# Rotary partner rows: eight TensorE products per layer replaced by copies between SBUF rows

## The chip, the cores and the metric

One core of a Trainium2 chip runs the whole program as one launch. The metric is the device time of that launch in microseconds. The kernel before was run three times; the median is 3442.33 us. One further execution was taken with the profiler, and its rows are the ones read here.

## What is computed

The reference is a stack of transformer layers over 512 tokens of width 1024, in f32: two layers of one block (their mixers are the kernel's `even` and `odd` phases, each between two feed-forward phases) and two layers of a second block. The change is in the token mixer of the second block, the kernel's `mix2` phase, which runs twice. Cut to what matters:

```
def apply_axial_rope(x, cos, sin):          # d = 64 (grouped heads) or 32 (latent heads)
    d = x.shape[-1]; h = d // 2; q = h // 2
    xr, xc = x[..., :h], x[..., h:]
    rot = lambda z: concatenate([-z[..., q:], z[..., :q]], axis=-1)
    x_rot = concatenate([rot(xr), rot(xc)], axis=-1)
    return x * cos + x_rot * sin

def token_mixer(u, ...):
    qa, ka, va, cq, ckv, kr, gl = split(u @ w_in)
    qa = apply_axial_rope(rmsnorm(qa, q_norm_g), cos_a, sin_a)      # 8 heads of 64
    ka = apply_axial_rope(rmsnorm(ka, k_norm_g), cos_a, sin_a)      # 2 heads of 64
    ya = blocked_attention(qa, ka, va)
    q_nope, q_rope = split(rmsnorm(cq, q_a_norm_g) @ w_q_up)        # 8 heads of 64 + 32
    k_nope, vb     = split(rmsnorm(ckv, kv_a_norm_g) @ w_kv_up)
    yb = blocked_attention([q_nope, rope(q_rope)], [k_nope, rope(kr)], vb)
    return merge of (ya, yb) with sigmoid gates, times w_o
```

The rotary step needs, for every row of a query or key, its partner row: 16 rows away for a head of 64, 8 rows away for a head of 32, with a sign.

## The kernel before

Activations lie with features on the 128 SBUF rows (partitions) and the 512 tokens along the free dimension, so one head pair is a tile of 128 x 512. Every f32 weight product is three TensorE passes: the weight block is split by ScalarE into a rounded high part (`round_to`, L381) and by GpSimd into the rest (`rest_block`, L408); SyncE loads the blocks (`load`, L360) through a ring of six slots. A load waits until TensorE is done with the block six places earlier, and `round_ahead` lets ScalarE round five blocks ahead of the item in hand, so at each item ScalarE waits for a load that starts when the block of the item before is done.

The front part of `mix2` follows a list written by hand, `ORDER2` (its rows stand below with the code), which all engines walk in the same order:

- `cq`, `kv`, `qk`, `kr`, `va`: projections of the input, one weight block each (three passes over eight row blocks on TensorE at L419 to L421). VectorE copies each result out of PSUM with the norm's factor (`b_qk` at L2503, `b_kr` at L2508, `b_vt` at L2510).
- `sum`: sums of squares for the norms, small matmuls at L2255 and L2258, from squares that ScalarE makes (L2417). After the third and the last `sum` ScalarE takes a square root (L2396) and VectorE a reciprocal (L2488).
- `spread`: the inverse norms of the latents and of the grouped keys spread over rows; VectorE applies them.
- `rot` 0 to 3 (grouped queries), `rot` 4 (grouped keys), `rotkr` (shared rotary key), `rotup` 0 and 1 (rotary part of the latent queries): the rotary step. TensorE multiplies the tile by a 128 x 128 matrix of signs (L2299: `b_rot` for the queries, which holds the norm's gain as well, or a part of `b_tab`) into one of five PSUM banks; VectorE multiplies that by the sine table into `work` (L2541), multiplies the tile by the cosine table in place (L2544 or L2547) and adds (L2548). That is eight rotary steps in a layer, sixteen in the program.
- `upr`, `upn`, `kn`: the latent queries and keys from their ranks (L2310 to L2312, L2321 to L2323), copied out by VectorE (L2555, L2561). `turn` transposes the grouped values.

PSUM is used in turn: a product that goes to tile n waits until VectorE has copied out tile n - 5 (`acc_free`). At the end TensorE waits for the copy of the last `kn` tile and for all eight rotary steps, and starts the attention (L1255), whose first operands ScalarE rounds (L2387) and VectorE splits (L2565). ScalarE issues no DMA in this phase; in the whole program it issues four, at the start.

Of the kernel before, what the change touches and what calls it, by code (L numbers as in the profile page):

```python
# [22 lines left out]
P = 128  # L23
S = 512
# [150 lines left out]
def build(nc, t, stop=99):  # L175
    with ExitStack() as ctx:
# [65 lines left out]
        mid2 = [("b_qk", [P, RAWS, S], F32), ("b_va", [P, S], F32), ("b_rot", [P, P], F32), ("gap2", [P, 2 * S - P], F32)]  # L242
        b_tab, b_small, c_hi, c_lo, b_qk, b_va, b_rot, _, b_qn, b_qr, b_kn, b_kr, b_vb = over(
# [48 lines left out]
        side_done, raw_copied, rotated = sem("side_done"), sem("raw_copied"), sem("rotated")  # L292
        tables_loaded, odd_loaded = sem("tables_loaded"), sem("odd_loaded")
# [1839 lines left out]
        COS_A, SIN_A, COS_B, SIN_B, ROT_A, ROT_B = 0, S, 2 * S, 3 * S, 4 * S, 4 * S + P  # L2133
# [12 lines left out]
        ROTS2 = [item for item in ORDER2 if item[0] in ("rot", "rotkr", "rotup")]  # L2146
        SIDES2 = 3 + 1
# [40 lines left out]
        def mix2_sp(sp, c, i):  # L2188

            def tables():  # L2190
                sp.wait_ge(blocks_done, block_done(c.blocks - 1))
                sp.dma_start(b_tab[:], t["tab_b"]).then_inc(tables_loaded, 16)
# [12 lines left out]
        def mix2_end(c):  # L2205
            c.blocks += len(mix2_blocks())
            c.tiles += len(TILES2)
            c.add("side", SIDES2 + len(ROTS2))
# [30 lines left out]
        def mix2_pe(pe, c, e):  # L2239
# [23 lines left out]
            for kind, i in ORDER2:  # L2263
# [206 lines left out]
        def mix2_dve(dve, ch, c):  # L2470
# [5 lines left out]
            for kind, i in ORDER2:  # L2476
# [8 lines left out]
                if kind == "sum":  # L2485
# [3 lines left out]
                    if i == GQ + 3:  # L2489
                        dve.wait_ge(rstd2_ready, c.at("rstd2") + 2)  # L2490
                        ch.link(dve.tensor_scalar(stat[:, 1, 8:40], stat[:, 0, 0:32], -HD ** -0.5, None, ALU.mult))
                        ch.link(dve.tensor_scalar(stat[:, 0, 0:32], stat[:, 0, 0:32], HD ** -0.5, None, ALU.mult))
                if kind in STEPS2:
# [6 lines left out]
                if (kind, i) == ("qk", 4):  # L2500
                    ch.link(dve.tensor_scalar(b_rot[:], b_tab[:, ROT_A:ROT_A + P], b_small[:, 0:1], None, ALU.mult))
# [33 lines left out]
                elif kind in ("rot", "rotkr", "rotup"):  # L2535
                    side, rots = side + 1, rots + 1
                    dst, _ = rotated_tile(kind, i)
                    cos, sin = (COS_A, SIN_A) if kind == "rot" else (COS_B, SIN_B)
                    dve.wait_ge(side_done, side)
                    dve.wait_ge(rotated, rots - 1)  # L2540
                    dve.tensor_tensor(work[:, 0, :], src[:], b_tab[:, sin:sin + S], ALU.mult).then_inc(acc_drained, 1)  # L2541
                    if kind == "rot" and i < 4:
                        dve.wait_ge(x_squared, c.at("sq") + NORMS2.index(("qk", i)) + 1)
                        ch.link(dve.scalar_tensor_tensor(out=dst, in0=dst, scalar=b_small[:, 0:1],  # L2544
                                                         in1=b_tab[:, COS_A:COS_A + S], op0=ALU.mult, op1=ALU.mult))
                    else:
                        ch.link(dve.tensor_tensor(dst, dst, b_tab[:, cos:cos + S], ALU.mult))  # L2547
                    dve.tensor_tensor(dst, dst, work[:, 0, :], ALU.add).then_inc(rotated, 1)  # L2548
# [287 lines left out]

def rotation(n, width, first=0):
# [5 lines left out]
    return r  # L2843


def second_table():
# [8 lines left out]
    a, b = np.tile(angles(HD), (2, 1)), angles(32)  # L2855
    b = np.tile(b, (4, 1))
    return np.concatenate([np.cos(a), np.sin(a), np.cos(b), np.sin(b), rotation(P, 32), rotation(P, 16)], 1).astype(f)


def lay_out(a):  # L2860
# [50 lines left out]
    a_cols = np.concatenate([np.arange(HD) + HD * head for j in range(4) for head in (j, j + 4)])  # L2911
    ins, ups, kvs, gates, outs, smalls, fup, fdown = ([] for _ in range(8))
    for i in range(2):
        w = a["w_in_2"][i]
        kr = np.tile(w[:, 1408:1440], (1, 4))
        ins.append(tiles_of(np.concatenate([w[:, 768:1408], w[:, 512:640], w[:, a_cols], kr, w[:, 640:768]], 1)))
        up = a["w_q_up_2"][i].reshape(QR * P, 8, QK)
        nope, rope = np.split(tiles_of(np.concatenate([up[:, :, :HD].reshape(QR * P, -1), up[:, :, HD:].reshape(QR * P, -1)], 1)), [4])
# [8 lines left out]
        smalls.append(np.concatenate([np.tile(a["q_norm_g_2"][i], 2)[:, None], np.tile(a["k_norm_g_2"][i], 2)[:, None],  # L2927
                                      columns(a["q_a_norm_g_2"][i]), columns(a["kv_a_norm_g_2"][i]),
                                      np.zeros((P, 1), np.float32), columns(a["b_gate_2"][i])], 1))
# [20 lines left out]
```

## Time and profile before

| | |
|---|---|
| median of three runs | 3442.33 us (3440.7 to 3442.33) |
| the profiled execution, whole | 3441.55 us |
| its span, first to last instruction | 3439.7 us |
| TensorE busy | 3400.9 us, 99% of the span |
| VectorE, GpSimd, ScalarE busy | 2087.8 us, 1989.7 us, 1530.3 us |
| granted TensorE clock, mean | 0.998 |

The front parts of `mix2` that the change touches lie at about 2000 to 2074 us and 2729 to 2805 us from the span's start. The program waits for TensorE nearly everywhere, so an instruction taken off TensorE counts fully unless TensorE then waits for something else. Matmuls overlap at their ends, so what one costs is read from the distance of starts. In the profile each f32 rotary matmul appears as two (x2).

### The profile page before, as it was taken

The numbers are of one execution on the slowest core, as the hardware profiler recorded it, in microseconds if no ns is written. First come the engines' busy times: TensorE is split into PE (matmuls) and PEld (weight loads), VectorE is DVE, ScalarE is ACT, GpSimd is POOL, SyncE is SP. The second block draws the span as 40 slices with busy tenths as digits, with TensorE's granted clock in tenths as the row PEclk, the third lists the DMA queues.
The fourth block names the chain that finished last, engine by engine and source line by source line (L and its number), as shares of the span: only waits on it lengthen the run. The fifth ranks groups of instructions, "written<-read, shape, count | busy, mean of one in ns | idle before, by whom it ended". The sixth has DMA issues, their size and how long they took to land. (4 is left out here: it accounts for less than half of the span.)

```text
span 3439.7 us, 46281 instructions
## 1 busy us (share of the span) xinstructions
PE 3400.9 (99%) x17572; PEld 2761.2 (80%) x17572; DVE 2087.8 (61%) x2990; ACT 1530.3 (44%) x2388; POOL 1989.7 (58%) x2338
## 2 busy tenths in 40 slices
PE   9999999999999999999999999999999999999999
PEld 8888868888888888748888887788788876888887
DVE  5556666655764468766645667326767575238667
ACT  4334454333533355675333537434444555335444
POOL 6555645555655658745665557554655665546564
PEclk9999999999999999999999999999999999999999
DMA  4223203233222322202332220123222210232321
GB/s 173 89 77 117 85 20 118 79 110 111 86 98 91 130 70 93 71 1 83 123 111 103 83 76 26 56 92 123 98 98 92 86 59 8 93 105 92 114 107 62
DMA packets 87726, 301.56 MB, mean 88 GB/s; under 512 B 9936, under 2 KB 14544, under 8 KB 87120
## 3 DMA queue, kind: packets, MB, share of 16 engines
q1 hardware_dynamic: 85392, 296.50, 24.4%
q8 instruction: 140, 2.29, 0.3%
q10 hardware_dynamic: 2112, 2.10, 0.2%
q14 instruction: 82, 0.67, 0.1%
HBM read 296.46 MB, written 2.10 MB: 87 GB/s over the span
## 5 line engine op out<-in xcount | busy, mean ns | idle before, releaser
L408 POOL TENSOR_TENSOR w_lo<-w_raw,w_hi 128x256 fp32r<-128x256 f32 x1754 | 1364.6, 812 | 1091.5 <-ACT w_hi L381 841.9
L419 PE MATMUL bank<-xh,w_hi 128*128 128x512 f32 x2544 | 997.8, 392 | 3.9 <-issue 1.5
L421 PE MATMUL bank<-xh,w_lo 128*128 128x512 f32 x2544 | 989.2, 389 | 0.0
L420 PE MATMUL bank<-xl,w_hi 128*128 128x512 f32 x2544 | 989.2, 389 | 0.0
L381 ACT ACTIVATE w_hi<-w_raw 128x1024 fp32r<-128x1024 f32 (+2 forms) x485 | 498.5, 1039 | 671.3 <-DMA w_raw<-in_ffn_up 269.3
L419 PEld LDWEIGHTS bank<-xh,w_hi 128*128 128x128 f32 x2544 | 478.1, 188 | 106.5 <-issue 4.6
L420 PEld LDWEIGHTS bank<-xl,w_hi 128*128 128x128 f32 x2544 | 478.2, 188 | 99.7 <-issue 2.4
L421 PEld LDWEIGHTS bank<-xh,w_lo 128*128 128x128 f32 x2544 | 478.0, 188 | 99.5
L408 POOL TENSOR_TENSOR extra_lo<-extra_raw,w_hi 128x256 fp32r<-128x256 f32 x264 | 229.8, 905 | 126.1 <-ACT w_hi L381 113.1
L1099 DVE TENSOR_TENSOR y_tok<-y_tok,bank 128x512 f32<-128x512 f32 x232 | 157.4, 685 | 223.1 <-PE bank L978 223.1
L1133 DVE TENSOR_TENSOR work<-bank,sqsum 128x512 f32<-128x512 f32 x88 | 60.7, 690 | 267.7 <-PE bank L421 267.7
L1025 ACT ACTIVATE ph<-work 128x1024 fp32r<-128x1024 f32 x76 | 80.7, 1062 | 299.1 <-DVE work L1113 299.1
L1379 POOL TENSOR_TENSOR work<-work,red 128x1024 f32<-128x1024 f32 (+2 forms) x88 | 151.3, 1721 | 88.5 <-DVE red L1325 88.5
L976 PE MATMUL bank<-w_hi,ph 128*128 128x512 f32 x512 | 200.0, 391 | 1.5 <-DVE work L1140 1.5
L978 PE MATMUL bank<-w_hi,pl 128*128 128x512 f32 x512 | 199.3, 389 | 0.0
L408 POOL TENSOR_TENSOR extra_lo<-extra_raw,x_hi 128x256 fp32r<-128x256 f32 x120 | 130.8, 1125 | 47.8 <-ACT x_hi L381 47.8
L381 ACT ACTIVATE w_hi<-extra_raw 128x1024 fp32r<-128x1024 f32 (+1 forms) x98 | 95.1, 1000 | 110.9 <-PE bank L978 107.4
L976 PE MATMUL bank<-w_hi,sh 128*128 128x512 f32 x360 | 140.5, 390 | 2.0 <-DVE sl L1121 1.2
L978 PE MATMUL bank<-w_hi,sl 128*128 128x512 f32 x360 | 140.1, 389 | 0.0
L1309 DVE TENSOR_REDUCE red<-scores 128x2 f32<-128x1024 f32 (+2 forms) x88 | 97.9, 1112 | 60.4 <-PE scores L1277 40.7
L642 PE MATMUL bank<-xh,w_hi 128*128 128x256 f32 x480 | 126.9, 293 | 2.4 <-ACT xh L602 2.4
L643 PE MATMUL bank<-xh,w_lo 128*128 128x256 f32 x480 | 123.3, 286 | 0.0
(454 smaller groups left out, 6154.2 us busy)
## 6 DMA issues: line engine op xcount, KB each, us to landing
w_raw<-in_ffn_up SPq DMA_DIRECT2D x176, 512.0 KB, 3.5
w_raw<-in_b_ffn_up SPq DMA_DIRECT2D x64, 512.0 KB, 3.5
extra_raw<-in_ffn_down SPq DMA_DIRECT2D x52, 512.0 KB, 4.5
w_raw<-in_b_gates SPq DMA_DIRECT2D x48, 512.0 KB, 3.4
extra_raw<-in_b_ffn_down SPq DMA_DIRECT2D x40, 512.0 KB, 4.5
w_raw<-in_od_in SPq DMA_DIRECT2D x33, 512.0 KB, 3.5
w_raw<-in_b_in SPq DMA_DIRECT2D x24, 512.0 KB, 3.6
w_raw<-in_ffn_down SPq DMA_DIRECT2D x20, 512.0 KB, 3.4
```

The lines of the kernel that those rows point to most:

```text
L381: act.activation(hi_of(g, whole(g)), src, ACT.Copy).then_inc(w_rounded, 1)
L408: ins = pool.tensor_tensor(lo_of(g, part), raw_of(g, part), hi_of(g, part).bitcast(F32), ALU.subtract)
L419: pe.matmul(out, wh, hi, start=first, stop=False)
L420: pe.matmul(out, wh, lo, start=False, stop=False)
L421: return pe.matmul(out, wl, hi, start=False, stop=last)
L642: pe.matmul(out, hi_of(B + j, cols), xh[:, k, half(h)], start=k == 0, stop=False)
L643: pe.matmul(out, lo_of(B + j, cols), xh[:, k, half(h)], start=False, stop=False)
L976: pe.matmul(out[:], hi, hi_of(block, cols), start=opens, stop=False, skip_group_check=True)
L978: mm = pe.matmul(out[:], lo, hi_of(block, cols), start=False, stop=ends, skip_group_check=True)
L1099: ins = dve.tensor_tensor(to, to, src, ALU.add)
L1309: ch.link(dve.reduce_max(r[:, 0:2], scores[g % 2][:, :, 0:u["keys"]], mybir.AxisListType.X))
L1379: pool.tensor_tensor(p, p, red[:, g % 4, 8:10].unsqueeze(2).broadcast_to([P, 2, u["keys"]]), ALU.mult)\
```

## The change

The eight rotary products of a layer leave TensorE. In their place ScalarE issues DMAs that copy each group of rows of the tile to the partner's rows of a new buffer `b_partner`, two tiles of 128 x 512 used in turn, and VectorE multiplies this by a sine table that now holds the sign. On the host the columns of the query and key weights (with their gains and tables) are put in another order, so that partners are 32 rows apart in a head of 64 and 16 in a head of 32: a `rot` tile takes four copies of 32 rows (64 KB each), the three others eight copies of 16 rows (32 KB each), 44 in a layer. Two semaphores, one for each buffer, count the landings. `MOVE_AT` names the item at which ScalarE issues each move; before a move it waits for the tile to be copied out and, from the third move on, for the rotary step two before. VectorE's three instructions of a step, and their place in `ORDER2`, stay; the first reads SBUF instead of PSUM. The product that made `b_rot` goes, and the table load loses the two sign matrices. ScalarE's rounding of the first grouped operands moves from the item `rotup` 0 to the item `upn` 1, behind the last move. The rotary tiles no longer take a turn in the five PSUM banks.

```
-        mid2 = [("b_qk", [P, RAWS, S], F32), ("b_va", [P, S], F32), ("b_rot", [P, P], F32), ("gap2", [P, 2 * S - P], F32)]
+        mid2 = [("b_qk", [P, RAWS, S], F32), ("b_va", [P, S], F32), ("b_partner", [P, 2, S], F32)]
...
-        STEPS2 = ("sum", "add")
+        STEPS2 = ("sum", "add", "rot", "rotkr", "rotup")
...
+        MOVE_AT = {("rot", 0): ("qk", 1), ("rot", 1): ("qk", 2), ("rot", 4): ("qk", 3), ("rot", 2): ("kr", 0), ("rotkr", 0): ("va", 0),
+                   ("rot", 3): ("va", 0), ("rotup", 0): ("upr", 1), ("rotup", 1): ("upn", 0)}
...
-                elif kind in ("rot", "rotkr", "rotup"):
-                    src, made = rotated_tile(kind, i)
-                    turn = b_rot[:] if kind == "rot" and i < 4 else b_tab[:, ROT_A:ROT_A + P] if kind == "rot" else \
-                        b_tab[:, ROT_B:ROT_B + P]
-                    pe.wait_ge(acc_drained, acc_free(tile))
-                    pe.wait_ge(acc_drained, drained(c.tiles + TILES2.index(made)))
-                    pe.wait_ge(tables_loaded, 48 + 32 * (c.at("tables") + 1))
-                    pe.matmul(out, turn, src, start=True, stop=True).then_inc(side_done, 1)
...
+            def move(r):
+                src, made = rotated_tile(*ROTS2[r])
+                wide = HD // 2 if ROTS2[r][0] == "rot" else 16
+                act.wait_ge(acc_drained, drained(T + TILES2.index(made)))
+                if r >= 2:
+                    act.wait_ge(rotated, c.at("rotated") + r - 1)
+                for to in range(0, P, wide):
+                    at = to + wide if to // wide % 2 == 0 else to - wide
+                    act.dma_start(b_partner[to:to + wide, r % 2, :], src[at:at + wide, :]).then_inc(partner_moved[r % 2], 16)
...
-                if (kind, i) == ("rotup", 0):
+                if (kind, i) == ("upn", 1):
                     act.wait_ge(rotated, c.at("rotated") + ROTS2.index(("rot", 3)) + 1)
                     round_grouped(act, 4)
                     round_grouped(act, 0)
...
                     round_ahead(act, g + (1 if g < c.blocks + OPEN else 0))
                     g += 1
+                for r, item in enumerate(ROTS2):
+                    if MOVE_AT[item] == (kind, i):
+                        move(r)
...
+                if kind in ("rot", "rotkr", "rotup"):
+                    r = ROTS2.index((kind, i))
+                    dst, _ = rotated_tile(kind, i)
+                    cos, sin = (COS_A, SIN_A) if kind == "rot" else (COS_B, SIN_B)
+                    dve.wait_ge(partner_moved[r % 2], moves(L, r))
+                    dve.wait_ge(rotated, rots)
...
+                        ch.link(dve.tensor_tensor(work[:, 0, :], b_partner[:, r % 2, :], b_tab[:, sin:sin + S], ALU.mult))
+                        ch.link(dve.tensor_tensor(dst, dst, b_tab[:, cos:cos + S], ALU.mult))
+                    dve.tensor_tensor(dst, dst, work[:, 0, :], ALU.add).then_inc(rotated, 1)
```

The order of instructions shows it at two places. The first is TensorE at the end of the fourth query projection of the first `mix2`, before:

```order
L420 MATMUL bank<-xl,w_hi 128x512
L421 MATMUL bank<-xh,w_lo 128x512
L2299 MATMUL bank<-b_qk,b_tab 128x512
L2258 MATMUL bank<-meancol,work 128x2 x4
L419 MATMUL bank<-xh,w_hi 128x512
```

and in the changed kernel (its lines are numbered a little higher):

```order
L421 MATMUL bank<-xl,w_hi 128x512
L422 MATMUL bank<-xh,w_lo 128x512
L2266 MATMUL bank<-meancol,work 128x2 x4
L420 MATMUL bank<-xh,w_hi 128x512
L421 MATMUL bank<-xl,w_hi 128x512
```

The rotary product of the grouped keys is gone, and the sums of squares follow the projection directly. The second place is ScalarE from the square of the last query tile to the rounding of the grouped operands, before (L381 rounds a weight block, L2396 is the square root of the last sums):

```order
L2417 ACTIVATE work<-b_qk 128x512
L381 ACTIVATE w_hi<-w_raw 128x1024 x2
L2396 ACTIVATE stat<-bank 128x32
L381 ACTIVATE w_hi<-w_raw 128x1024 x2
L2387 ACTIVATE hi_a<-b_qk 128x512 x2
```

and in the changed kernel:

```order
L2430 ACTIVATE work<-b_qk 128x512
L382 ACTIVATE w_hi<-w_raw 128x1024
L2402 DMA b_partner<-b_qk 32x512 x4
L382 ACTIVATE w_hi<-w_raw 128x1024
L2402 DMA b_partner<-b_kr 16x512 x8
L2402 DMA b_partner<-b_qk 32x512 x4
L2406 ACTIVATE stat<-bank 128x32
L382 ACTIVATE w_hi<-w_raw 128x1024
L2402 DMA b_partner<-b_qr 16x512 x8
L382 ACTIVATE w_hi<-w_raw 128x1024
L2402 DMA b_partner<-b_qr 16x512 x8
L2387 ACTIVATE hi_a<-b_qk 128x512 x2
```

Thirty-two DMA issues now stand between ScalarE's own instructions here, twelve of them directly ahead of the square root.

## Rows read from the trace of the kernel before

**Rows 1.** The page's busy times, all engines, whole span.

```profile
PE 3400.9 (99%) x17572; PEld 2761.2 (80%) x17572; DVE 2087.8 (61%) x2990; ACT 1530.3 (44%) x2388; POOL 1989.7 (58%) x2338
```

**Rows 2.** TensorE's waits, first `mix2` front and the attention's start.

```profile
PE scores L1255 <- DVE b_kn L2561: 0.8, 1, 0.8
PE bank L2258 <- ACT work L2417: 0.8, 1, 0.8
```

**Rows 3.** Timeline, TensorE, first layer: start us, us, engine, line, operation [idle <-releaser].

```profile
2035.93 1.02 PE L2299 MATMUL bank<-b_qk,b_tab 128*128 128x512 f32 x2
2036.79 0.95 PE L2258 MATMUL bank<-meancol,work 128*128 128x2 f32 x8
...
2062.65 1.02 PE L2299 MATMUL bank<-b_qr,b_tab 128*128 128x512 f32 x2
...
2063.74 0.40 PE L2311 MATMUL bank<-c_lo,w_hi 128*128 128x512 f32 x1
2063.97 0.40 PE L2312 MATMUL bank<-c_hi,w_lo 128*128 128x512 f32 x1
...
2072.84 0.39 PE L2323 MATMUL bank<-c_hi,w_lo 128*128 128x512 f32 x1
2074.02 0.50 PE L1255 MATMUL scores<-hi_a 64*128 64x512 f32 x2 [0.78 <-DVE b_kn L2561]
```

**Rows 4.** Timeline, VectorE, first layer, the last rotary step to the attention.

```profile
2063.87 0.68 DVE L2541 TENSOR_TENSOR work<-bank,b_tab 128x512 f32<-128x512 f32 x1
2064.47 0.72 DVE L2547 TENSOR_TENSOR b_qr<-b_qr,b_tab 128x512 f32<-128x512 f32 x1
2065.22 1.12 DVE L2548 TENSOR_TENSOR b_qr<-b_qr,work 128x512 f32<-128x512 f32 x1
2066.26 0.68 DVE L2555 COPY b_qn<-bank 128x512 f32<-128x512 f32 x1
...
2073.27 0.69 DVE L2561 COPY b_kn<-bank 128x512 f32<-128x512 f32 x1 [0.65 <-PE bank L2323]
```

**Rows 5.** Timeline, ScalarE, first layer.

```profile
2021.23 0.63 ACT L2417 ACTIVATE work<-b_qk 128x512 f32<-128x512 f32 x1 [4.79 <-DVE b_qk L2503]
...
2046.83 1.06 ACT L381 ACTIVATE w_hi<-w_raw 128x1024 fp32r<-128x1024 f32 x1 [6.23 <-DMA w_raw<-in_b_kv]
2051.38 0.20 ACT L2396 ACTIVATE stat<-bank 128x32 f32<-128x32 f32 x1 [3.49 <-PE bank L2258]
2054.57 1.06 ACT L381 ACTIVATE w_hi<-w_raw 128x1024 fp32r<-128x1024 f32 x1 [2.99 <-DMA w_raw<-in_b_gates]
2060.92 1.06 ACT L381 ACTIVATE w_hi<-w_raw 128x1024 fp32r<-128x1024 f32 x1 [5.29 <-DMA w_raw<-in_b_gates]
```

**Rows 6.** Timeline, DMA issues of ScalarE's queue.

```profile
0.71 2.57 ACTq L2742 DMA_DIRECT2D x<-in_x  x4
```

**Rows 7.** Timeline, DMA issues of SyncE's queue, two stretches.

```profile
2043.35 0.33 SPq L360 DMA_DIRECT2D w_raw<-in_b_kv  x1
...
2359.55 1.87 SPq L360 DMA_DIRECT2D extra_raw<-in_b_ffn_down  x4
```

**Rows 8.** DMA issues by line: count, KB each, median us from issue to landing.

```profile
w_raw<-in_b_kv SPq DMA_DIRECT2D x4, 512.0 KB, 3.5
out_x<-x SPq DMA_DIRECT2D x16, 128.0 KB, 1.8
w_raw<-in_ffn_down SPq DMA_DIRECT2D x4, 256.0 KB, 2.5
b_small<-in_b_small SPq DMA_DIRECT2D x2, 12.0 KB, 6.8
```

**Rows 9.** Stretches (us; busy by engine; last three: granted clock, DMA share, GB/s).

```profile
2013.00:2076.00 63.00, 61.44 (x297) 47.97 (x297) 39.80 (x58) 20.18 (x29) 30.59 (x39) 1.00 0.23 77
2742.00:2806.00 64.00, 62.44 (x295) 48.75 (x294) 39.31 (x59) 19.91 (x28) 29.86 (x38) 0.97 0.22 73
...
2744.00:2748.00 4.00, 4.00 (x12) 3.08 (x12) 0.25 (x1) 1.12 (x3) 4.00 (x7) 0.57 0.00 0
```

More of the change, by code:

```diff
@@ L241, in build @@
         head2 = [("c_hi", [P, QR + KR, S], F32R), ("c_lo", [P, QR + KR, S], F32R)]
-        mid2 = [("b_qk", [P, RAWS, S], F32), ("b_va", [P, S], F32), ("b_rot", [P, P], F32), ("gap2", [P, 2 * S - P], F32)]
-        b_tab, b_small, c_hi, c_lo, b_qk, b_va, b_rot, _, b_qn, b_qr, b_kn, b_kr, b_vb = over(
+        mid2 = [("b_qk", [P, RAWS, S], F32), ("b_va", [P, S], F32), ("b_partner", [P, 2, S], F32)]
+        b_tab, b_small, c_hi, c_lo, b_qk, b_va, b_partner, b_qn, b_qr, b_kn, b_kr, b_vb = over(
             "hh", *tab2, *head2, *mid2, ("b_qn", [P, 4, S], F32), ("b_qr", [P, 2, S], F32), ("b_kn", [P, 4, S], F32),
@@ L292, in build @@
         side_done, raw_copied, rotated = sem("side_done"), sem("raw_copied"), sem("rotated")
+        partner_moved = [sem(f"partner_moved{i}") for i in range(2)]
         tables_loaded, odd_loaded = sem("tables_loaded"), sem("odd_loaded")
@@ L2146, in build, with moves, pieces @@
         ROTS2 = [item for item in ORDER2 if item[0] in ("rot", "rotkr", "rotup")]
+        MOVE_AT = {("rot", 0): ("qk", 1), ("rot", 1): ("qk", 2), ("rot", 4): ("qk", 3), ("rot", 2): ("kr", 0), ("rotkr", 0): ("va", 0),
+                   ("rot", 3): ("va", 0), ("rotup", 0): ("upr", 1), ("rotup", 1): ("upn", 0)}
+        def moves(layer, r):
+            def pieces(item):
+                return 4 if item[0] == "rot" else 8
+            return 16 * (layer * sum(map(pieces, ROTS2[r % 2::2])) + sum(map(pieces, ROTS2[r % 2:r + 1:2])))
         SIDES2 = 3 + 1
@@ L2207, in mix2_end @@
             c.tiles += len(TILES2)
-            c.add("side", SIDES2 + len(ROTS2))
+            c.add("side", SIDES2)
             c.add("rotated", len(ROTS2))
@@ L2492, in mix2_dve @@
                         ch.link(dve.tensor_scalar(stat[:, 0, 0:32], stat[:, 0, 0:32], HD ** -0.5, None, ALU.mult))
+                if kind in ("rot", "rotkr", "rotup"):
[4 more added lines that the diff above has]
+                    dve.wait_ge(rotated, rots)
+                    rots += 1
+                    if kind == "rot" and i < 4:
+                        ch.link(dve.scalar_tensor_tensor(out=work[:, 0, :], in0=b_partner[:, r % 2, :], scalar=b_small[:, 7:8],
+                                                         in1=b_tab[:, SIN_A:SIN_A + S], op0=ALU.mult, op1=ALU.mult))
+                        dve.wait_ge(x_squared, c.at("sq") + NORMS2.index(("qk", i)) + 1)
+                        ch.link(dve.scalar_tensor_tensor(out=dst, in0=dst, scalar=b_small[:, 0:1],
+                                                         in1=b_tab[:, COS_A:COS_A + S], op0=ALU.mult, op1=ALU.mult))
+                    else:
+                        ch.link(dve.tensor_tensor(work[:, 0, :], b_partner[:, r % 2, :], b_tab[:, sin:sin + S], ALU.mult))
+                        ch.link(dve.tensor_tensor(dst, dst, b_tab[:, cos:cos + S], ALU.mult))
+                    dve.tensor_tensor(dst, dst, work[:, 0, :], ALU.add).then_inc(rotated, 1)
                 if kind in STEPS2:
@@ L2534, in mix2_dve @@
                     dve.wait_ge(xl_ready, xn + j + 1)
[L2535 to L2548, printed above, removed]
                 elif kind in ("upr", "upn"):
@@ L2834, in even_table, with turn_sign @@
     return np.concatenate([np.cos(ang), np.sin(ang), mask, pool, rotation(P, HD)], 1).astype(f)
+def turn_sign(width):
+    return np.where(np.arange(P) % width < width // 2, -1, 1)[:, None]
 def rotation(n, width, first=0):
@@ L2843, in rotation, with turned_order @@
     return r
+def turned_order(dim):
+    return np.arange(dim).reshape(2, 2, dim // 4).transpose(1, 0, 2).reshape(-1)
 def second_table():
@@ L2854, in angles @@
         return np.concatenate([r, r, c, c], 1).T.astype(f)
-    a, b = np.tile(angles(HD), (2, 1)), angles(32)
+    a, b = np.tile(angles(HD)[turned_order(HD)], (2, 1)), angles(32)[turned_order(32)]
     b = np.tile(b, (4, 1))
-    return np.concatenate([np.cos(a), np.sin(a), np.cos(b), np.sin(b), rotation(P, 32), rotation(P, 16)], 1).astype(f)
+    return np.concatenate([np.cos(a), turn_sign(HD) * np.sin(a), np.cos(b), turn_sign(32) * np.sin(b)], 1).astype(f)
 def lay_out(a):
@@ L2911, in lay_out @@
     a_cols = np.concatenate([np.arange(HD) + HD * head for j in range(4) for head in (j, j + 4)])
+    order_a, order_b = turned_order(HD), turned_order(32)
+    q_cols = np.concatenate([order_a + HD * head for j in range(4) for head in (j, j + 4)])
+    k_cols = np.concatenate([512 + order_a + HD * head for head in range(2)])
     ins, ups, kvs, gates, outs, smalls, fup, fdown = ([] for _ in range(8))
@@ L2914, in lay_out @@
         w = a["w_in_2"][i]
-        kr = np.tile(w[:, 1408:1440], (1, 4))
-        ins.append(tiles_of(np.concatenate([w[:, 768:1408], w[:, 512:640], w[:, a_cols], kr, w[:, 640:768]], 1)))
+        kr = np.tile(w[:, 1408 + order_b], (1, 4))
+        ins.append(tiles_of(np.concatenate([w[:, 768:1408], w[:, k_cols], w[:, q_cols], kr, w[:, 640:768]], 1)))
         up = a["w_q_up_2"][i].reshape(QR * P, 8, QK)
-        nope, rope = np.split(tiles_of(np.concatenate([up[:, :, :HD].reshape(QR * P, -1), up[:, :, HD:].reshape(QR * P, -1)], 1)), [4])
+        nope, rope = np.split(tiles_of(np.concatenate([up[:, :, :HD].reshape(QR * P, -1), up[:, :, HD + order_b].reshape(QR * P, -1)], 1)), [4])
         ups.append(np.concatenate([rope, nope]).transpose(1, 0, 2).reshape(P, -1))
@@ L2926, in lay_out @@
         outs.append(tiles_of(a["w_o_2"][i]))
-        smalls.append(np.concatenate([np.tile(a["q_norm_g_2"][i], 2)[:, None], np.tile(a["k_norm_g_2"][i], 2)[:, None],
+        q_gain, k_gain = a["q_norm_g_2"][i][order_a], a["k_norm_g_2"][i][order_a]
+        smalls.append(np.concatenate([np.tile(q_gain, 2)[:, None], np.tile(k_gain, 2)[:, None],
                                       columns(a["q_a_norm_g_2"][i]), columns(a["kv_a_norm_g_2"][i]),
-                                      np.zeros((P, 1), np.float32), columns(a["b_gate_2"][i])], 1))
+                                      np.tile(np.roll(q_gain, HD // 2), 2)[:, None], columns(a["b_gate_2"][i])], 1))
         fup.append(tiles_of(a["w_ffn_up_2"][i]))
```

6 lines of the change are left out of this document (2 added, 4 removed).

## The prediction

> **What bounds the kernel now.** I read the page's busy times first: TensorE is busy 99% of the span, the others 44 to 61% [rows 1]. So the kernel is TensorE's list of instructions, and what leaves it is a gain as long as TensorE finds no new wait. The waits come next: in the front of the first `mix2` TensorE waits twice, 0.8 us each, once for a square and once, ahead of the attention, for VectorE's copy of the last latent keys [rows 2]; the second layer has the same two. VectorE and ScalarE follow so closely that the front is near a second bound, and that is what the timelines are read for. The last matmul of the front and the first of the attention show the 0.78 us of waiting [rows 3]. VectorE's last rotary step ends at 2066.3, its last copy starts at 2073.27 as soon as its product is there, and ScalarE idles for 3 to 6 us between its weight roundings, most of it for loads [rows 4, 5].
>
> **What leaves TensorE.** One rotary product takes 2036.79 - 2035.93 = 0.86 us between starts; where a projection follows, the second matmul behind it stands 1.09 us later, and less one step of 0.23 that is 0.86 again [rows 3]. Read so, the eight of a layer cost 0.86 to 0.95, 7.15 us in all, and the sixteen 14.3 us. If nothing else changed the front would end 7.15 us earlier in each layer. The product that made `b_rot` (once a layer) stands ahead of several us of idle VectorE time and counts as nothing; if that time were gone it would cost what a short VectorE instruction costs. The shorter table load counts as nothing too: it is issued before the mixer's projections.
>
> **What ScalarE gets.** In a layer five moves of four DMAs and three of eight. No row shows an issue of 16 or 32 rows of SBUF, so the price is bounded by the nearest ones. SyncE's single issue takes 0.33 us and four in a row take 1.87, 0.47 each [rows 7]; ScalarE's own four, of larger pieces at the start, take 2.57, 0.64 each [rows 6]. I take 0.37 for the first and 0.44 for each further one: nearest to SyncE's four in a row, a little less because a piece has a quarter or an eighth of the rows, if rows matter. That is 1.7 us for four, 3.45 for eight. Ends for the range: 0.33 and 0.64. For the landing I take 1.8 us from the start of the last issue, the row of 128 KB [rows 8]; sizes of 256 and 512 KB take 2.5 and 3.5, so little is left to gain with size. Below, a landing of 1.0 would give 0.8 us more a layer; above stands the 6.8 us of a 12 KB load that was queued behind a large one.
>
> Here the Trainium skill speaks otherwise: "DMA: Bandwidth & Descriptors", under "Issuing engines are not separate DMA queues", says that the sequencer's time to start a DMA is usually small relative to the DMA itself. By that rule the sum would be the whole 14.3 us. The rows speak against it for pieces as small as these: four issues together take as long as one landing [rows 6 to 8].
>
> **The path.** I followed the engines' lists in order with these durations (without the change this reproduces the first layer's front within 0.3 us). VectorE's own three instructions per step stay, 2.5 us with their gaps [rows 4]; the first now reads SBUF only, and I give it 0.1 us more.
>
> The moves of `rot` 0 and 1 are hidden: ScalarE idles 4.79 us ahead of a square there [rows 5]; without it the square, and the sums behind it, would come 1.7 us later. Those of `rot` 4 and 2 land about 0.9 us after VectorE is ready, which VectorE's idle time ahead of the next two projections takes up.
>
> From `va` on it binds. TensorE is now 3.6 us early. ScalarE rounds the block whose load starts at the end of `kr`: before at 2046.83 [rows 5], now at about 2044.1, done at 2045.1. Then come twelve issues, 5.15 us, and the square root behind them runs at 2050.3 instead of 2051.38, though its sums are ready at 2047.6: 2.5 of the 3.6 us are lost. Behind it VectorE waits, since the reciprocal stands ahead of its `rotkr` step, that ahead of the copy of `upr` 0, and this is what ScalarE's next move waits for. The copy is done at 2054.1; eight issues to 2057.6, landed at 2058.9, half a us after VectorE needs them; `rotup` 0 done at 2061.5. ScalarE rounds a block (1.06) and issues the last eight from 2058.6 to 2062.0, landed at 2063.4; VectorE has waited 1.3 us, and ends the last step at 2065.9, hardly earlier than the 2066.3 of before. What is gained comes behind it: eight instructions of about 0.62 us that were spread over TensorE's `kn` products, up to 2073.27 [rows 4], now follow each other, and end at 2070.9. TensorE meanwhile stands twice, 2.2 us ahead of its last `kn` tile (the copy of five tiles before is late) and 3.0 us behind it. The attention begins at about 2071.2 instead of 2074.02 [rows 3]: 2.8 us gained per layer of the 7.15.
>
> **The clock.** In the second layer TensorE's granted clock was 0.57 in one stretch of 4 us, 1.2 instead of 2.4 GHz for most of it, and not in the first, where the whole front shows 1.00 [rows 9]. Ahead of that fall stood small matmuls and the 0.8 us wait. It cost 0.43 of 4 us, 1.7 us. The 2.2 and 3.0 us waits with one short product between them leave TensorE idle for longer, so I count a fall at the attention's start in each layer: 3.4 us. Bounds: none (0), or these and no second-layer fall (-1.7 more gained).
>
> **The sum**, against the profiled execution's own time, which is 0.78 us under the median: 3441.55 - 2 x 2.8 + 2 x 1.7 = 3439.3 us. The attention and all behind it are the same list of instructions; the turn of the five banks shifts, but no wait on a bank shows there.
>
> **Rivals.** All are measured against the median; about 0.2%, 6.9 us, is what a measurement of this kernel can tell from no change.
>
> *The issues cost next to nothing*, and ScalarE's moves vanish between its roundings. Then VectorE is never late and TensorE gains all: 3441.55 - 14.3 = 3427.3 us. For it: ScalarE's idle time and the small pieces. Against it: the four issues in a row of either queue [rows 6, 7]. Chance 0.15. The rule of the Trainium skill quoted above would have it so.
>
> *Slower: ScalarE's issues cost what its own row says*, 0.64 each. Place: the twelve issues ahead of the square root (7.7 us) and the two eights (5.1 us each) behind it, one chain through VectorE. The same walk gives 2.85 us lost per layer, with the two falls of the clock 3441.55 + 5.7 + 3.4 = 3450.7 us. It decides from about 0.49 us per issue, where gain and clock cancel. For it: it is this engine's only row [rows 6]. Against it: those were 512 KB pieces, issued while SyncE issued six. Chance 0.14.
>
> *The landings are late*, because the copies share the 16 engines with weight loads of 3.5 us [rows 8]. At 4 us a layer loses 0.3: 3445.6 us with the falls; at 5.2 it loses 3.6: 3452.2 us. For it: a weight load is under way in about half the front. Against it: the copies have ScalarE's own queue, and each is small. Chance 0.18.
>
> **How the numbers follow.** The forecast, chance 0.53, covers issues of 0.37 to 0.48 us, 4.4 to 1.9 us per layer, with none to two falls: 3432.7 to 3441.2 us. Faster by over 0.2% (below 3435.4) are the first rival and a fifth of the forecast: 0.26. Slower by over 0.2% (above 3449.2) are most of the second and about 0.07 of the third: 0.20. The rest, 0.54, is within. The range, 3429 to 3451, leaves out the first rival's end and the worst landings: issues of 0.33 (5.8 per layer) without a fall give 3430.0, the slow rival 3450.7.
>
> **What would show it.** Right: rows of four and eight issues on ScalarE's queue of 1.5 to 1.9 and 3.2 to 3.8 us; the second square root about 1 us earlier while its sums stand ready; VectorE waiting for DMA ahead of its last two steps; TensorE waiting some 2 and 3 us at the last `kn` tile and the attention; a granted clock well under 1 there. Wrong: no new wait on TensorE (first rival), issues of 0.6 us, or landings of 4 us and more.

## The result, and the profile after

The changed kernel takes 3449.44 us (median of 16 runs, 3447.66 to 3452.38) against 3442.19 us (16 runs, 3440.13 to 3444.07) for the kernel before in the same comparison: ratio 1.0021, 95% interval 1.0014 to 1.0029. It is slower by 7.25 us, a little more than the 0.2% that the prediction named as measurable, and not 3 us faster. The profiled execution took 3447.66 us with a span of 3445.9 us.

The page's busy times after, to be held against [rows 1]:

```profile
PE 3390.6 (98%) x17540; PEld 2755.2 (80%) x17540; DVE 2090.1 (61%) x2988; ACT 1530.0 (44%) x2388; POOL 2000.2 (58%) x2338
```

TensorE works 10.3 us less than before and the span is 6.2 us longer, so some 16 us of new waiting replaced the products. TensorE's waits in the first `mix2` front of the changed kernel (us in total, times, longest) show where:

```profile
PE bank L2321 <- DVE b_qn L2569: 4.7, 2, 2.7
PE scores L1256 <- DVE b_kn L2575: 2.7, 1, 2.7
PE bank L2310 <- DVE b_qr L2569: 2.6, 2, 1.6
PE bank L2266 <- ACT work L2430: 0.8, 1, 0.8
```

Before there were two waits of 0.8 us [rows 2]. Now there are 10.0 us ahead of VectorE's copies, more than the 7.15 us of products that went. VectorE is late because ScalarE is. ScalarE's timeline in the changed kernel, from the item `va` on:

```profile
2043.96 4.99 ACTq L2402 DMA_DIRECT2D b_partner<-b_kr  x8
2049.05 3.44 ACTq L2402 DMA_DIRECT2D b_partner<-b_qk  x4
2052.53 0.20 ACT L2406 ACTIVATE stat<-bank 128x32 f32<-128x32 f32 x1 [7.85 <-issue]
...
2057.18 5.00 ACTq L2402 DMA_DIRECT2D b_partner<-b_qr  x8
2062.22 1.06 ACT L382 ACTIVATE w_hi<-w_raw 128x1024 fp32r<-128x1024 f32 x1 [8.55 <-DVE b_qn L2569]
2062.30 5.00 ACTq L2402 DMA_DIRECT2D b_partner<-b_qr  x8
```

Eight issues take 5.0 us. The square root (L2406) waits for nothing but the issues ahead of it: TensorE's last sums of squares began at 2045.84 and took 0.95 us, the root ran at 2052.53. VectorE's timeline in the same stretch shows what follows from it:

```profile
2052.76 0.35 DVE L2501 RECIPROCAL stat<-stat 128x32 f32<-128x32 f32 x1 [5.70 <-ACT stat L2406]
...
2063.60 1.05 DVE L2520 TENSOR_TENSOR work<-b_partner,b_tab 128x512 f32<-128x512 f32 x1 [1.91 <-DMA b_partner<-b_qr]
...
2068.71 0.69 DVE L2520 TENSOR_TENSOR work<-b_partner,b_tab 128x512 f32<-128x512 f32 x1 [1.19 <-DMA b_partner<-b_qr]
2069.43 0.69 DVE L2521 TENSOR_TENSOR b_qr<-b_qr,b_tab 128x512 f32<-128x512 f32 x1
2070.16 1.10 DVE L2522 TENSOR_TENSOR b_qr<-b_qr,work 128x512 f32<-128x512 f32 x1
2071.18 1.27 DVE L2569 COPY b_qn<-bank 128x512 f32<-128x512 f32 x2
...
2074.91 1.28 DVE L2575 COPY b_kn<-bank 128x512 f32<-128x512 f32 x2
```

It stands 5.70 us for the reciprocal and 1.91 and 1.19 us for the landings of the last two moves. The last rotary step ends at 2071.3 (2066.3 before, [rows 4]), the last copy at 2076.2. TensorE's timeline:

```profile
2067.58 0.50 PE L2321 MATMUL bank<-c_hi,w_hi 128*128 128x512 f32 x1 [1.97 <-DVE b_qn L2569]
2071.92 0.49 PE L2321 MATMUL bank<-c_hi,w_hi 128*128 128x512 f32 x1 [2.68 <-DVE b_qn L2569]
2076.24 0.49 PE L1256 MATMUL scores<-hi_a 64*128 64x512 f32 x2 [2.67 <-DVE b_kn L2575]
```

The span can be cut where TensorE starts the third sum of squares (`sum` GK, the last point that the moves cannot reach) and where it starts the attention, in each layer:

| stretch, us | before | after | difference |
|---|---|---|---|
| start to sums, layer 1 | 2013.82 | 2012.63 | -1.2 |
| front, sums to attention, layer 1 | 60.20 | 63.61 | +3.4 |
| attention to sums, layer 2 | 668.84 | 671.93 | +3.1 |
| front, layer 2 | 61.79 | 64.26 | +2.5 |
| attention of layer 2 to the end | 635.05 | 633.47 | -1.6 |

The two fronts lose 5.9 us together. Of the 3.1 us between them 1.6 are a clock fall right behind the attention's start: from 2078.5 to 2081.1 TensorE's starts stand 0.43 us apart instead of 0.23 (the stretches from 2076 to 2084 below), and the second scores follow the first after 6.09 us instead of 4.53. Another 1.5 us are an idle gap of TensorE with no releaser, which is not the change's: each of the eleven profiles has it once, behind one of the two attentions. In the changed kernel it stands behind the first, in the kernel before behind the second, where it makes the -1.6 of the last row:

```profile
2192.84 0.47 PE L420 MATMUL bank<-xh,w_hi 128*128 128x512 f32 x1 [1.47 <-issue]
```

```profile
2919.86 0.47 PE L419 MATMUL bank<-xh,w_hi 128*128 128x512 f32 x1 [1.47 <-issue]
```

The -1.2 of the first row lies ahead of the moves, and nothing here explains it.

### The profile page after: what moved, and what is told of

It reads as the page before. It is cut to its first block, busy times and chain, and to the rows that moved or that the text cites. A ratio compares the mean times of both kernels' runs of the same rounds, so it can differ in the third digit from the quotient of the medians.

```text
span 3445.9 us, 46307 instructions
## 1 busy us (share of the span) xinstructions
PE 3390.6 (98%) x17540; PEld 2755.2 (80%) x17540; DVE 2090.1 (61%) x2988; ACT 1530.0 (44%) x2388; POOL 2000.2 (58%) x2338
## 4 chain that ended last, share of the span: by engine, by line
PE 48%; DVE 5%; POOL 2%; ACTq 1%; issue 1%; ACT 1%; DMA 0%; DVEq 0%; POOLq 0%
PE bank L420 9%; PE bank L422 9%; PE bank L421 9%; PE bank L977 3%; PE bank L979 3%; PE bank L978 3%; PE bank L1294 2%; PE bank L1271 2%; PE scores L1256 2%; POOL extra_lo L409 2%; ACTq L2402 1%; PE bank L2366 1%; PE bank L2367 1%; PE bank L2368 1%; PE bank L1747 1%
```

## The experiments

The theory: ScalarE's price of an issue, about 0.61 us, 44 times a layer, made the loss. Rival 1: the way out of VectorE's tile through a DMA and back costs what it costs, however many pieces and whoever issues. Rival 2: only the falls of the clock in TensorE's new waits count. The kernel before ran beside each; every ratio is to it.

| kernel | median us (range, runs) | before | ratio, 95% interval |
|---|---|---|---|
| e1 two issues a move | 3431.47 (3428.13 to 3437.62, 7) | 3441.83 | 0.9973, 0.9962 to 0.9983 |
| e2 issued by SyncE | 3442.87 (3440.1 to 3447.26, 11) | 3441.83 | 1.0005, 0.9996 to 1.0015 |
| e3 64 issues a layer | 3460.99 (3459.09 to 3463.32, 5) | 3441.83 | 1.0057, 1.0044 to 1.007 |
| e4 `rot` alone | 3432.17 (3431.36 to 3433.11, 7) | 3441.83 | 0.9972, 0.9961 to 0.9983 |
| e5 `rot` 3 behind the root | 3446.82 (3445.03 to 3449.92, 11) | 3442.16 | 1.0014, 1.0006 to 1.0023 |
| e6 waits filled | 3447.51 (3444.51 to 3448.74, 11) | 3442.16 | 1.0014, 1.0006 to 1.0023 |
| e7 e1 + `kn` copies by ScalarE | 3431.42 (3430.3 to 3432.92, 5) | 3442.16 | 0.9968, 0.9955 to 0.998 |
| e8 `rotkr`, `rotup` alone | 3452.42 (3451.1 to 3455.34, 7) | 3442.16 | 1.0029, 1.0018 to 1.004 |
| e9 e1 + `upn` copies by ScalarE | 3427.93 (3425.43 to 3428.18, 5) | 3441.3 | 0.9961, 0.9948 to 0.9975 |

**e1, the same bytes in 16 issues a layer instead of 44.**

```
-    return np.arange(dim).reshape(2, 2, dim // 4).transpose(1, 0, 2).reshape(-1)
+    return np.arange(dim).reshape(2, 2, dim // 4).transpose(0, 2, 1).reshape(-1)
...
-                for to in range(0, P, wide):
-                    at = to + wide if to // wide % 2 == 0 else to - wide
-                    act.dma_start(b_partner[to:to + wide, r % 2, :], src[at:at + wide, :]).then_inc(partner_moved[r % 2], 16)
+                for s in range(2):
+                    act.dma_start(b_partner[s:P:2, r % 2, :], src[1 - s:P:2, :]).then_inc(partner_moved[r % 2], 16)
```

> The order of the columns is changed once more, so that a row's partner is the next row (the sine table's signs and the gains follow). A move is then two DMAs by ScalarE, 64 rows each at a step of two rows, instead of four or eight: 16 issues in a layer instead of 44, with the same bytes, the same issuing engine and the same places. Theory (ScalarE's issue price, 0.61 us each, is what turned the gain into a loss): ScalarE is rid of 28 x 0.61 = 17 us per layer, VectorE is no longer late, and nearly all of the 14.3 us of rotary products comes out: 3428 us, up to 3431.5 if TensorE's clock still falls. Rival 1 (the way out and back counts, VectorE to DMA to VectorE, 2.1 us however many pieces): as the change, 3447 to 3450. Rival 2 (only the clock falls count): not below 3442 as long as TensorE waits at the start of the attention.

Measured 3431.47 us, at the theory's upper figure, and 3428.13 in the profiled execution. Rival 1 falls: the moves still go out through a DMA and back. ScalarE's timeline of e1 at the place of the twelve issues:

```profile
2043.16 1.12 ACTq L2400 DMA_DIRECT2D b_partner<-b_kr  x2
2044.55 1.12 ACTq L2400 DMA_DIRECT2D b_partner<-b_qk  x2
2046.73 0.20 ACT L2404 ACTIVATE stat<-bank 128x32 f32<-128x32 f32 x1 [2.56 <-PE bank L2266]
```

The root now waits for TensorE's sums and not for issues, and comes 5.8 us earlier. Of TensorE's waits in the front two are left, 0.8 and 1.7 us. Rival 2's "not below 3442" falls too. The spread of 9.5 us goes with the mean granted clock of the runs, 0.999 in the fastest and 0.996 in the slowest; where the falls lay, the one profile, taken in the fastest run, cannot show.

**e2, the 44 pieces issued by SyncE.** The move's body stands in SyncE's list, each behind a weight load:

```
+            behind = {0: [0], 1: [1], 2: [2], 3: [3], 4: [4, 5], 5: [6], 6: [7]}
...
+                load(sp, g + j, src)
+                for r in behind.get(j, []):
+                    move(r)
```

> The same 44 pieces in a layer, issued by SyncE: each move directly behind the weight load that SyncE issues at about that time; it waits there for the same two semaphores. ScalarE has no moves. Theory: SyncE issues these pieces in 0.33 to 0.47 us each, so with landings of 2.1 us the front gains 2.0 us per layer, 3442.2 - 4.0 + 3.4 (clock) = 3441.6 us; with landings of 4 us, if a piece waits behind the 512 KB load ahead of it in the same queue, 0.7 us lost per layer, 3447. In both cases the second square root comes as soon as its sums are ready. Rival 1 (the way out and back): 3447 to 3450, with the square root early and VectorE just as late. If the price belongs to the piece (SBUF to SBUF, 16 or 32 rows) and not to the engine, SyncE's rows show 0.61 too and the time is as the change, 3449.

The expectation was wrong on the price and the time lay at its smaller figure. SyncE's timeline of e2:

```profile
2043.46 4.93 SPq L2213 DMA_DIRECT2D b_partner<-b_kr  x8
2048.49 2.43 SPq L2213 DMA_DIRECT2D b_partner<-b_qk  x4
2050.97 1.59 SPq L361 DMA_DIRECT2D w_raw<-in_b_gates  x1
2054.19 4.93 SPq L2213 DMA_DIRECT2D b_partner<-b_qr  x8
2059.17 0.58 SPq L361 DMA_DIRECT2D w_raw<-in_b_gates  x1
```

Eight issues cost SyncE 4.93 us, hardly less than ScalarE's 5.0; even a weight load right behind them costs 0.58, once 1.59, instead of the 0.33 of [rows 7]. So the price is not ScalarE's own. The expectation's last case had this price, but a time as the change's with it, and the time did not follow. What the issuer decides is who stands behind the issues. Here ScalarE's root was punctual (2048.93, released by TensorE's sums), and VectorE waited 2.42 and 2.87 us for the landings of the two `rotup` moves; the kernel gains 6.6 us on the change and ends level with the kernel before. In exchange the weight loads stand behind the moves: ScalarE's rounding waits up to 6.5 us for one, without holding TensorE up.

**e3, 20 more issues a layer.**

```
-                for to in range(0, P, wide):
+                for to in range(0, P, 16):
...
-                    act.dma_start(b_partner[to:to + wide, r % 2, :], src[at:at + wide, :]).then_inc(partner_moved[r % 2], 16)
+                    act.dma_start(b_partner[to:to + 16, r % 2, :], src[at:at + 16, :]).then_inc(partner_moved[r % 2], 16)
```

> The five rot moves of a layer in eight pieces of 16 rows instead of four of 32: 20 more issues per layer by ScalarE, the same bytes, places and waits otherwise. Theory: 20 x 0.61 = 12.2 us more on ScalarE per layer, of which some 8 us reach the path (the walk through the lists): 3449.4 + 16 = 3465 us. Rival 1: a move comes back as before, 3448 to 3452. Rival 2: as the change, since TensorE's number of waits is the same, 3449 to 3452.

Measured 3460.99 us, 11.6 us above the change for 40 more issues; both rivals said none. The size, 16 us expected, was too large. In the profiled executions the spans are 13.3 us apart; the fronts, 68.28 and 69.27 us, are 4.7 and 5.0 above the change's, where the theory had some 8 each. (The second difference is 6.6 without a clock fall of 1.6 us at the third sum of squares, which the change has in that layer and e3 has not; see e6.) The rows of the pieces (count, ns as min, median and max), first of the change and then of e3, say that halving a piece does not cheapen it:

```profile
L2402 ACTq DMA_DIRECT2D b_partner<-b_qk x40: 514/612/1576, 2014.2 to 2787.8; - x40
```

```profile
L2402 ACTq DMA_DIRECT2D b_partner<-b_qk x80: 514/611/1301, 2015.5 to 2798.6; - x80
```

and in e1, with 64 rows in a piece, it is not dearer:

```profile
L2400 ACTq DMA_DIRECT2D b_partner<-b_qk x20: 472/559/932, 2014.2 to 2769.6; - x20
```

**e4 and e8, one half of the change each.** In e4 the five `rot` steps are moved and the rest are products again; in e8 it is the other way round. The core of e4, and of e8:

```
-        STEPS2 = ("sum", "add", "rot", "rotkr", "rotup")
+        STEPS2 = ("sum", "add", "rot")
+        MOVED2 = [item for item in ROTS2 if item[0] == "rot"]
```

```
-        STEPS2 = ("sum", "add", "rot", "rotkr", "rotup")
+        STEPS2 = ("sum", "add", "rotkr", "rotup")
+        MOVED2 = [item for item in ROTS2 if item[0] != "rot"]
```

> Only the five rot steps of a layer (grouped queries and keys) are moved, four issues each by ScalarE as in the change; rotkr and the two rotup steps are TensorE products again, with the column order of before for the latent heads. Theory: the 20 issues lie beside ScalarE's idle time and none stands ahead of the last two steps, so the five products come out, 4.5 us per layer: 3442.2 - 9.0 = 3433.2 us. Rival 1 (way out and back): rot 2 and rot 3 are still late by a landing each; VectorE makes up for that, 3433 to 3436. Rival 2 (clock): the waits at the attention's start are short as in the kernel before, so no fall there: 3433. If the first five moves already cost what they save, 3442.

> The converse of moving the five rot steps alone: these are TensorE products again (with the column order of before for the heads of 64), and rotkr and the two rotup steps are moved, eight issues each by ScalarE, 24 in a layer. Theory: eight issues stand ahead of the second square root, and rotup's two eights each on the path between a copy and VectorE's step; by the walk 3.1 us lost per layer although three products are gone: 3442.2 + 6.2 = 3448.4, up to 3452 with clock falls at the attention's start. Rival 1 (the way out and back): 3442 to 3446. If the five rot moves carried the loss: 3437, the three products saved.

Measured 3432.17 us for e4 (expected 3433.2) and 3452.42 us for e8 (expected 3448.4, up to 3452 with clock falls). The 20 issues for `rot` are covered by ScalarE's idle time; the 24 of the other three steps are not, and cost more than the whole change. TensorE's waits in the first front of e4 are those of before:

```profile
PE scores L1256 <- DVE b_kn L2588: 0.8, 1, 0.8
PE bank L2265 <- ACT work L2435: 0.8, 1, 0.8
```

VectorE's timeline of e8 shows it late at each of the three moves, and not mainly for the root:

```profile
2052.66 0.35 DVE L2507 RECIPROCAL stat<-stat 128x32 f32<-128x32 f32 x1 [0.80 <-ACT stat L2412]
2055.87 0.69 DVE L2518 TENSOR_TENSOR work<-b_partner,b_tab 128x512 f32<-128x512 f32 x1 [2.42 <-DMA b_partner<-b_kr]
2066.68 1.10 DVE L2518 TENSOR_TENSOR work<-b_partner,b_tab 128x512 f32<-128x512 f32 x1 [3.31 <-DMA b_partner<-b_qr]
2071.55 0.69 DVE L2518 TENSOR_TENSOR work<-b_partner,b_tab 128x512 f32<-128x512 f32 x1 [0.90 <-DMA b_partner<-b_qr]
```

**e5, eight issues ahead of the root instead of twelve.**

```
-                   ("rot", 3): ("va", 0), ("rotup", 0): ("upr", 1), ("rotup", 1): ("upn", 0)}
+                   ("rot", 3): ("upr", 0), ("rotup", 0): ("upr", 1), ("rotup", 1): ("upn", 0)}
```

> One entry of the table that names the place of each move: the move of rot 3 is issued at upr 0 instead of va, behind the second square root. The same 44 issues by ScalarE, in another order: eight instead of twelve ahead of the root. Theory: the root, and VectorE's reciprocal behind it, come 4 x 0.61 = 2.4 us earlier; rot 3 itself comes later; by the walk through the lists the layer gains 1.9 us: 3449.4 - 3.8 = 3445.6 us. Rival 1 (the way out and back of each move) and rival 2 (the clock falls alone): nothing changes, 3449.

Measured 3446.82 us, 2.6 us below the change where 3.8 were expected, and still above the kernel before. ScalarE's order matters, as the theory has it; VectorE's wait for the root falls from 5.70 to 2.26 us, and it then waits 2.19 us for `rotkr`'s move and 2.48 for the first `rotup`'s.

**e6, TensorE's new waits filled with small products.**

```
+                    idle_pe(pe, bank[7], {("upn", 2): 2, ("upn", 3): 4}.get((kind, i), 0))
                     pe.wait_ge(acc_drained, acc_free(tile))
...
+                    idle_pe(pe, bank[7], (0, 0, 8, 9)[i])
                     pe.wait_ge(acc_drained, acc_free(tile))
...
+            idle_pe(pe, bank[7], 6)
             pe.wait_ge(acc_drained, drained(c.tiles + len(TILES2) - 1))
```

> The change, and TensorE fills its new waits with small products into a bank that is free there: 2, 4, 8, 9 and 6 products of 128x128 ahead of upn 2, upn 3, kn 2, kn 3 and the attention, some 0.2 us each, so that each fills about the wait that the change's trace shows there. Rival 2 (only the clock falls count): the granted clock stays 1.00 at the attention's start in both layers and the whole loss goes, below 3442. Theory: only the clock's share comes back, 1.7 us in the first layer and 1.7 to 3.4 in the second, 3444 to 3446 us, above the kernel before, since VectorE is as late as it was. If the falls don't depend on these waits: 3449.

Measured 3447.51 us: 1.9 us less than the change, less than expected, and 5.3 above the kernel before. Rival 2 falls. Stretches of the change around the attention's start in both layers (us; busy time by engine; then granted clock, DMA share, GB/s):

```profile
2072.00:2076.00 4.00, 1.57 (x6) 0.96 (x6) 4.00 (x7) 2.45 (x4) 4.00 (x5) 1.00 0.31 111
2076.00:2080.00 4.00, 3.76 (x17) 2.77 (x18) 2.88 (x5) 1.30 (x3) 2.19 (x3) 0.71 0.06 23
2080.00:2084.00 4.00, 4.00 (x17) 2.71 (x17) 2.21 (x4) 2.79 (x7) 3.14 (x2) 0.86 0.00 0
...
2804.00:2808.00 4.00, 1.90 (x6) 0.95 (x5) 3.04 (x5) 3.09 (x5) 2.30 (x3) 0.59 0.04 8
2808.00:2812.00 4.00, 2.93 (x6) 1.82 (x6) 4.00 (x8) 2.64 (x5) 4.00 (x6) 0.56 0.00 0
```

and of e6:

```profile
2076.00:2080.00 4.00, 2.69 (x23) 2.07 (x22) 2.94 (x6) 0.76 (x2) 4.00 (x5) 1.00 0.45 135
2080.00:2084.00 4.00, 4.00 (x21) 2.70 (x19) 3.57 (x7) 3.00 (x6) 1.59 (x2) 1.00 0.00 0
...
2804.00:2808.00 4.00, 3.51 (x24) 3.06 (x24) 2.94 (x4) 3.08 (x5) 2.21 (x2) 1.00 0.04 8
2808.00:2812.00 4.00, 2.99 (x18) 2.54 (x18) 4.00 (x8) 2.74 (x5) 4.00 (x6) 1.00 0.22 63
```

In the change TensorE was busy for 1.57 of the 4 us ahead of the first fall to 1.2 GHz; with the waits filled the clock stays at 2.4 GHz there. Not every fall costs. The second layer's lay ahead of the attention, where TensorE was waiting for VectorE anyway, and it took its time from that wait, which is 1.40 us there and 2.67 in the first layer:

```profile
2812.43 0.50 PE L1256 MATMUL scores<-hi_a 64*128 64x512 f32 x2 [1.40 <-DVE b_kn L2575]
```

The fronts can be compared only with a second kind of fall taken out, the one at the third sum of squares. The change meets it in its second layer, as the kernel before does [rows 9], and e6 in its first. The stretch behind the second layer's third sum, of the change and then of e6:

```profile
2748.00:2752.00 4.00, 3.83 (x17) 3.29 (x18) 0.25 (x1) 2.40 (x5) 2.86 (x5) 0.76 0.37 114
```

```profile
2748.00:2752.00 4.00, 3.25 (x18) 2.86 (x19) 0.25 (x1) 3.01 (x5) 2.52 (x5) 1.00 0.40 115
```

With this fall TensorE goes from the third sum to the fourth in 15.55 us, without it (the change's first layer) in 13.92. The change's second front, 64.26 us, is 62.6 without it, and e6's is 63.79: the fall ahead of the attention shows no price of its own.

**e7 and e9, is VectorE what is left?** Both start from e1 and let ScalarE copy two tiles out of PSUM, e7 `kn` 2 and 3, e9 `upn` 2 and 3. VectorE skips these copies. ScalarE's list in e7, and in e9:

```
+                if kind == "kn" and i >= 2:
...
+                    act.wait_ge(acc_drained, drained(T + n - 1))
+                    act.activation(b_kn[:, i, :], bank[(T + n) % ACCS][:], ACT.Copy).then_inc(acc_drained, 1)
```

```
+                if kind == "upn" and i >= 2:
...
+                    act.wait_ge(acc_drained, drained(T + n - 1))
+                    act.activation(b_qn[:, i, :], bank[(T + n) % ACCS][:], ACT.Copy).then_inc(acc_drained, 1)
```

> The kernel with neighbouring partners and two issues per move, and besides ScalarE copies the last two kn tiles out of PSUM in VectorE's place (VectorE is busy without a gap there, ScalarE is idle half of the time). Theory: TensorE's wait ahead of the attention falls from 1.7 and 2.7 us to about 0.8, as in the kernel before; with it the last cause of a clock fall there: 3428.1 (its best run) - 2.9 = 3425 to 3428 us in every run. If the falls come without that wait too, the spread of 3428 to 3437 stays.

> The kernel with neighbouring partners and two issues per move, and ScalarE copies the upn 2 and upn 3 tiles out of PSUM in VectorE's place; the two kn copies tried before stood behind ScalarE's roundings of the grouped queries and came no earlier, these stand ahead of them. VectorE is rid of 1.2 us behind the last rotary step. Theory: its last kn copy ends about 0.8 us behind the last kn product and TensorE's wait ahead of the attention is 0.8 us in both layers instead of 1.7 and 2.7; without falls of the clock at the attention 3428.1 - 2.8 = 3425.3 us for the best run, and a median of 3427 to 3429 with the fall of 1.7 us that some layer shows at the third sum of squares in nearly every run. If VectorE's list is not what ends the front, 3431.5 as before this edit.

e7 missed: 3431.42 us, as e1. Its wait ahead of the attention is 1.9 us, now for ScalarE, whose copies stood behind a rounding that waited for a load until 2062.93 and behind the roundings of the grouped queries:

```profile
2063.89 1.13 ACT L2387 ACTIVATE hi_a<-b_qk 128x512 fp32r<-128x512 f32 x2
2064.93 0.61 ACT L2387 ACTIVATE hi_b<-b_qk 128x512 fp32r<-128x512 f32 x1
2065.45 1.27 ACT L2426 ACTIVATE b_kn<-bank 128x512 f32<-128x512 f32 x2
```

e9 gave 3427.93 us (expected 3427 to 3429), 13.4 us below the kernel before beside it, and beats both kernels. VectorE's timeline of e9 has a gap again ahead of its last copy, as in [rows 4]:

```profile
2064.52 0.69 DVE L2580 COPY b_kn<-bank 128x512 f32<-128x512 f32 x1 [0.32 <-PE bank L2323]
```

Its fronts take 53.26 and 53.82 us.

## Why the prediction was wrong

**The products: right.** e9's first front ends with the same wait of 0.8 us as the kernel before and is 60.20 - 53.26 = 6.9 us shorter; 7.15 was forecast.

**The landings: right where it counts.** Forecast 1.8 us, measured 2.0 to 2.1 for most pieces, 2.7 for `rotkr`'s. The last pieces of the two `rotup` moves, for which VectorE waits, landed after 2.0. Single pieces took up to 4.0 us, the third rival's figure, such as the last of `rot` 2; VectorE's wait for that one ends ahead of its longer wait for the root. The third rival is out as the cause.

**The price of an issue: the step that failed.** The prediction took "0.37 for the first and 0.44 for each further one: nearest to SyncE's four in a row, a little less because a piece has a quarter or an eighth of the rows". Measured 0.51 and 0.61 on ScalarE, which with the short gaps between them makes 5.0 us for eight where 3.45 were forecast, and 2.5 for four where 1.7 were. Both reasons for the lower value were wrong. The rows hardly matter (medians of 0.61 for 16 and for 32 rows and 0.56 for 64, where half the issues are first ones: e3, change, e1), and SyncE's four loads [rows 7] were no measure even of SyncE: these pieces cost it 0.51 to 0.59 (e2). The nearest row was ScalarE's own, 0.64 with the gaps [rows 6], which the text discounted for its large pieces. The twelve issues ahead of the root were forecast at 5.15 us. They took 7.6 in the second layer and 8.5 in the first, where one of them took 1.58. The second layer:

```profile
2780.90 5.00 ACTq L2402 DMA_DIRECT2D b_partner<-b_kr  x8
2785.99 2.47 ACTq L2402 DMA_DIRECT2D b_partner<-b_qk  x4
2788.51 0.20 ACT L2406 ACTIVATE stat<-bank 128x32 f32<-128x32 f32 x1 [6.60 <-issue]
```

**The path: right in its places.** The root behind twelve issues, VectorE's reciprocal behind it, the two `rotup` moves and TensorE's waits at `kn` and the attention all appeared. The forecast's times count from the kernel before, and the changed kernel reached the third sum 1.2 us earlier (2012.63 against 2013.82). Allowing for that, the root was forecast at 2049.1 and ran at 2052.53; the last rotary step was to end at 2064.7 and ended at 2071.3; the last copy at 2069.7 and ended at 2076.2. TensorE's waits, 2.2 and 3.0 us in the forecast, were 2.0, 2.7 and 2.7, with 2.6 more ahead of the `upn` products. The fronts lose 3.4 and 2.5 us where a gain of 2.8 each was forecast.

In the first layer that is 6.2 us, about what the issues took beyond the forecast on this chain: 3.4 us for the twelve and 1.6 for each eight. Two smaller terms were off too and cancel. From the root to the end of the copy of `upr` 0 passed 4.6 us instead of 3.8, since VectorE's `rotkr` step took longer. And the last eight issues began 0.1 us behind the first eight instead of 1.0, since they ran beside ScalarE's rounding (2062.22, 1.06 us) and did not wait for its end.

The loss is the second rival's, 2.85 per layer and 3450.7 us, though that sum has one costly fall of the clock too many. Its point of decision, 0.49 us an issue, lies between the forecast price and the measured one. e1, e3, e4 and e8 bear it out: the time follows the number of issues and their place. In e1 VectorE's two `rotup` steps take 3.0 us each, against 2.6 and 2.5 in the kernel before, and it gains all the same, so longer steps of VectorE did not make the loss.

**The clock: half right.** The falls came at the attention's start in both layers, and e6 shows that they hang on the waits; but a wait alone does not bring one, for e1 waits 2.7 us ahead of its second attention with the clock at 2.4 GHz. Two were counted at 1.7 us each; the one behind the first attention's start cost 1.6, the other nothing that shows. The sum with the measured terms is 3441.55 + 5.9 + 1.6 = 3449.1 us, against a median of 3449.44. That it comes so close is in part luck: the profiled execution, from which the terms are read, took 3447.66 us, because it was also 1.2 us quicker ahead of the moves.

The rule of the Trainium skill, "DMA: Bandwidth & Descriptors", section "Issuing engines are not separate DMA queues", that the time to start a DMA is usually small relative to the DMA, is borne out here only in part. One piece's issue took 0.51 to 0.61 us of the 2.0 to 2.1 to its landing, over a quarter, and a chain of eight issues took 5.0 us. The prediction had 3427.3 us by this rule; only e9, with two issues a move and a lighter VectorE, came there.

**Left open.** Why four loads in a row cost SyncE 0.47 us each with their gaps, eight of these pieces 0.62, and a load behind them 0.58; why one issue took 1.58 us; why VectorE's `rotkr` step took longer; and why the third sum of squares meets a fall of the clock in one layer (the kernel before, the change, e2, e4, e6, e7, e8), in both (e5) or in none (e1, e3, e9), with the same wait of 0.8 us. None of these was tried.

## What to carry to other kernels

Count the DMA issues, not the bytes: here each held its engine's list for 0.5 to 0.6 us whether it moved 16 rows or 64, and what stands behind it in that engine's list pays. Choose the data layout so that a move takes the fewest issues; a layout that puts partners on neighbouring rows lets a step of two rows do it in two. A move between one engine's copy and its next step is a chain of issues plus a landing (for eight pieces 5.0 - 0.6 us to the start of the last issue, and 2.1 more), and is cheap only where that engine has other work for as long.

## What was not expected of the hardware

A piece of 16, 32 or 64 rows (the last at a step of two rows) costs ScalarE about the same to issue, 0.5 us for the first and 0.6 for a further one, and lands in 2.0 to 2.1 us. SyncE issues a single weight load in 0.33 us [rows 7], but in 0.58 right behind a chain of small ones, and such chains cost it as much as ScalarE. ScalarE's issues run beside an activation that is already under way (eight began at 2062.30, 0.08 us behind the start of a rounding of 1.06 us), but the next activation waits for all of them. A fall of TensorE's clock to 1.2 GHz cost 1.6 us where TensorE had products to run, and nothing that shows where it ended in a wait for VectorE.
